# An HGRN2 recurrence in two groups of four heads, its output projection split over K, and overflow tables in whole passes

## What is computed

```python
def hgrn2(h, w_in, lb, o_norm_g, w_out):     # 8 heads of 128
    q, f, i, g = jnp.split(h @ w_in, 4, axis=-1)
    forget = lb + (1.0 - lb) * jax.nn.sigmoid(f)
    log_f, k, q = jnp.log(forget), 1.0 - forget, jax.nn.silu(q)
    ...
    def step(state, inp):                    # over chunks of 64 frames
        qc, kc, ic, lfc = inp
        b = jnp.cumsum(lfc, axis=2)
        o_inter = jnp.einsum('bhtk,bhkv->bhtv', qc * jnp.exp(b), state)
        ...
        o = o_inter + jnp.einsum('bhts,bhsv->bhtv', attn, ic)
        ...
    o = rms_norm(o, o_norm_g)                # per head
    return (o * jax.nn.silu(g)) @ w_out

x = x + rms_norm(mix, norm_g[layer, 1])
hn = rms_norm(x, norm_g[layer, 2])
logits = hn @ w_router + b_router            # then top 2 of 8, softmax, the experts
```

## Time and profile before

| | us |
|---|---|
| median of 3 runs | 1562.08 (1562.06 to 1563.52) |
| the profiled execution | 1561.03 |
| its span, first to last instruction | 1559.2 |
| TensorE busy | 1510.1 (97%) |
| DVE busy | 1277.6 (82%) |
| ACT busy | 1005.7 (64%) |
| DMA queue of the weights | 435.25 MB, 76.4% of 16 engines |

### The profile page before, as it was taken

How to read it: one execution, slowest core, us unless ns; L and a number is a source line. 1 busy time by engine, 2 the same in 40 slices (tenths; PEclk the granted TensorE clock), 3 DMA queues, 4 the chain that set the end, 5 groups by cost and what they waited for, 6 DMA issues and landing times.

```text
span 1559.2 us, 24123 instructions
## 1 busy us (share of the span) xinstructions
PE 1510.1 (97%) x7090; PEld 1257.1 (81%) x7101; DVE 1277.6 (82%) x1595; ACT 1005.7 (64%) x1274; POOL 10.7 (1%) x26
## 2 busy tenths in 40 slices
PE   7999999999979899999999999999999999999998
PEld 6777888788867688888888888888888888887876
DVE  6986455674877898999988989899999889998985
ACT  6555444464323577777767867777777777776772
POOL 1000000000000000000000000000000000000000
PEclk9999999999989899999999999999999999999999
DMA  7666555363322699989989989989989998998960
GB/s 279 205 226 216 190 185 185 114 217 119 111 81 95 246 365 368 366 330 371 353 327 381 355 329 372 370 310 380 377 307 379 379 349 330 372 351 330 378 259 28
DMA packets 121236, 439.93 MB, mean 282 GB/s; under 512 B 13664, under 2 KB 13664, under 8 KB 121200
## 3 DMA queue, kind: packets, MB, share of 16 engines
q1 hardware_dynamic: 119952, 435.25, 76.4%
q0 software_dynamic: 1248, 4.23, 0.7%
HBM read 438.38 MB, written 1.05 MB: 282 GB/s over the span
## 4 chain that ended last, share of the span: by engine, by line
PE 90%; DVE 6%; ACT 2%; issue 1%; DMA 1%; SPq 0%; DVEq 0%; ACTq 0%
PE PS L397 28%; PE PS L399 27%; PE PS L398 27%; DVE w_lo L1200 2%; PE PS L631 2%; PE PS L761 2%; PE PS L721 1%; DMA raw<-in_w_in_ab 1%; PE PS L735 1%; DVE xT_lo L1669 1%; ACT xT_hi L1106 0%; PE PS L736 0%; ACT w_hi L862 0%; PE PS L447 0%; ACT xT_hi L877 0%
## 5 line engine op out<-in xcount | busy, mean ns | idle before, releaser
L1200 DVE TENSOR_TENSOR w_lo<-raw,w_hi 128x1024 fp32r<-128x1024 f32 x486 | 567.8, 1221 | 34.4 <-ACT w_hi L862 31.5
L397 PE MATMUL PS<-w_hi,xT_hi 128*128 128x512 f32 x1424 | 566.1, 398 | 6.5 <-DVE xT_lo L1268 3.5
L399 PE MATMUL PS<-w_lo,xT_hi 128*128 128x512 f32 x1424 | 556.9, 391 | 0.0
L398 PE MATMUL PS<-w_hi,xT_lo 128*128 128x512 f32 x1424 | 555.9, 390 | 0.0
L862 ACT ACTIVATE w_hi<-raw 128x1024 fp32r<-128x1024 f32 x486 | 490.0, 1061 | 74.7 <-PE PS L399 49.1
L1200 DVE TENSOR_TENSOR w_lo<-SC,w_hi 128x1024 fp32r<-128x1024 f32 x340 | 391.3, 1220 | 11.5 <-ACT w_hi L862 10.5
L862 ACT ACTIVATE w_hi<-SC 128x1024 fp32r<-128x1024 f32 x340 | 337.5, 1060 | 34.2 <-PE PS L399 31.5
L397 PEld LDWEIGHTS PS<-w_hi,xT_hi 128*128 128x128 f32 x1424 | 269.3, 189 | 61.7 <-issue 3.9
L399 PEld LDWEIGHTS PS<-w_lo,xT_hi 128*128 128x128 f32 x1424 | 268.3, 188 | 57.7
L398 PEld LDWEIGHTS PS<-w_hi,xT_lo 128*128 128x128 f32 x1424 | 268.9, 189 | 53.6
L397 PE MATMUL PS<-w_hi,hT_hi 128*128 128x512 f32 x536 | 208.9, 390 | 4.1 <-DVE hT_lo L1405 4.1
(11 more groups left out here) (235 smaller groups left out, 722.9 us busy)
## 6 DMA issues: line engine op xcount, KB each, us to landing
raw<-in_e_w_gu SPq DMA_DIRECT2D x226, 512.0 KB, 6.7
SC<-in_e_w_gu SPq DMA_DIRECT2D x222, 512.0 KB, 6.7
SC<-in_e_w_down SPq DMA_DIRECT2D x114, 512.0 KB, 5.8
raw<-in_e_w_down SPq DMA_DIRECT2D x110, 512.0 KB, 6.2
raw<-in_ffn_w_gu SPq DMA_DIRECT2D x44, 512.0 KB, 4.8
raw<-in_w_in_c SPq DMA_DIRECT2D x32, 512.0 KB, 5.6
raw<-in_ffn_w_down SPq DMA_DIRECT2D x22, 512.0 KB, 5.0
raw<-in_w_in_ab SPq DMA_DIRECT2D x20, 512.0 KB, 6.9
```

The lines of the kernel that those rows point to most:

```text
L397: pe.matmul(out, a_hi, b_hi, start=start, stop=False, skip_group_check=True)
L398: pe.matmul(out, a_lo, b_hi, start=False, stop=False, skip_group_check=True)
L399: return pe.matmul(out, a_hi, b_lo, start=False, stop=stop, skip_group_check=True)
L1200: dve.tensor_tensor(w_lo[:, g % RING, part], raw_part(g, s), w_hi[:, g % RING, part].bitcast(F32), ALU.subtract).then_inc(lo_done, 1)
```

## The change

Four edits.

1. The eight heads are two groups of four (`GH` = 4), with their own buffers, semaphores (`qk_ready_low`, `qk_ready_high`) and PSUM banks. The chunks of the input projection come in the order f of group 0, q of group 0, f of group 1, q of group 1, values and gates of group 0, values and gates of group 1 (`INC`). The levels of group 0 begin behind half-granule 5, those of group 1 behind half-granule 9.
2. The output projection is split over K: the half of group 0 for both chunks is done first, that of group 1 last, tile by tile. `turn_x(3, 0)` stands behind all of it. A head norm now ends in four fused products per group and tile instead of two whole passes, and the loads of the experts' fourth granule wait for the last of four head norms.
3. The overflow tables are made for all three extra places at once.
4. `xT_half` without a scale copies and subtracts four blocks in one instruction.

```diff
+            proj(4)
+            pe.wait_ge(q_evac, 1)
+            turn_heads(q_nat[0], 6, qT_psum)
             proj(5)
+            pe.wait_ge(qT_act, 2)
+            level(0, 0)
+            proj(6)
+            level(0, 1)
...
+            proj(13)
+            across(0)
+            weigh_values(0, 0)
+            level(1, 4)
+            pe.wait_ge(g_evac, 1)
+            proj(14)
+            weigh_values(0, 1)
+            level(1, 5)
             proj(15)
-            level(7)
+            level(1, 6)
+            for t in range(T):
+                turn_o(0, t)
+            pe.wait_ge(i_evac, 2)
+            for t in range(T):
+                out_seg(0, 0, t)
+            level(1, 7)
             pe.wait_ge(g_evac, 2)
+            out_seg(0, 1, 0)
+            across(1)
+            weigh_values(1, 0)
+            out_seg(0, 1, 1)
+            weigh_values(1, 1)
             for t in range(T):
+                turn_o(1, t)
+                for c in range(2):
+                    out_seg(1, c, t)
+            turn_x(3, 0)
```

The helpers of TensorE that are new or changed:

```diff
+            def across(g):
+
+                pe.wait_ge(qk_ready[g], 9)
+                for hd in range(GH):
+                    m = pe.matmul(PS[:, o_bank(g, 1), hd * P:(hd + 1) * P], kT[g][:, hd, 0:P], qT[g][:, hd, P:SEQ],
+                                  start=True, stop=True, skip_group_check=True)
+                m.then_inc(at_done[g], 1)
+
+            def weigh_values(g, t):
+
+                pe.wait_ge(qk_ready[g], 9 + t)
...
+            def turn_o(g, t):
+
+                pe.wait_ge(o_ready, T * g + t + 1)
+                for j in range(HK):
+                    m = pe.transpose(PS[:, o_bank(g, t), j * P:(j + 1) * P], oo[g][:, t, j * P:(j + 1) * P], ident[:, :])
+                m.then_inc(xT_psum, 1)
+
+            def out_seg(h, c, t):
+                g = G_OUTC + 2 * h + c
+                pe.wait_ge(xT_ready, 8 * T + T * h + t + 1)
+                seg(g, c, h, t, h == 0, h == 1, None, h == 1)
```

DVE's order in the same stretch (`climb` is one level of one group, `norm_o` one head norm):

```diff
+            crossed(0)
+            gains_of(0)
+            climb(1, 4)
+            norm_o(0, 0)
+            lo(68)
+            climb(1, 5)
+            norm_o(0, 1)
+            lo(69)
+            climb(1, 6)
+            lo(70)
             for t in range(T):
+                oT(0, t)
+            climb(1, 7)
+            lo(71)
+            gains_of(1)
+            crossed(1)
+            norm_o(1, 0)
+            norm_o(1, 1)
+            oT(1, 0)
+            oT(1, 1)
+            los(72, 74)
             for c in range(2):
                 dve.wait_ge(y_half, Y_OUTC + c + 1)
                 weigh_psum(0, c, 4)
```

The head norm on DVE, the whole-half split, and the loads on SP:

```diff
+            def norm_o(g, t):
+
+                heads = slice(HEADS * g + GH * t, HEADS * g + GH * (t + 1))
+                dve.wait_ge(o_sq, T * g + t + 1)
+                step(dve.tensor_reduce(rt[:, heads], osq[g][:, t, :].rearrange("p (h n) -> p h n", n=HD), AXX, ALU.add))
+                step(dve.tensor_scalar(nr[:, 0, heads], rt[:, heads], 1.0 / HD, EPS, ALU.mult, ALU.add))
+                rsqrt(heads.start, heads.stop)
+                for hd in range(GH):
+                    cols = slice(hd * HD, (hd + 1) * HD)
+                    m = dve.scalar_tensor_tensor(out=oo[g][:, t, cols], in0=PS[:, o_bank(g, t), cols],
+                                                 scalar=nr[:, 1, heads.start + hd:heads.start + hd + 1],
+                                                 in1=gg[g][:, t, cols], op0=ALU.mult, op1=ALU.mult)
+                m.then_inc(o_ready, 1)
...
+                if v is None:
+                    part = (slice(None), slice(HK * b, HK * (b + 1)), slice(t * P, (t + 1) * P))
+                    dve.tensor_tensor(xT_lo[part], PS[:, tile_bank(t, final) + b, :].rearrange("p (k c) -> p k c", k=HK),
+                                      xT_hi[part].bitcast(F32), ALU.subtract).then_inc(xT_ready, 1)
+                    return
...
-            for c in (2, 3, 0, 1, 4, 5, 6, 7):
+            for c in INC:
...
-                        sp.wait_ge(o_ready, T)
+                        sp.wait_ge(o_ready, 2 * T)
```

ACT's order at the end, and the new table code:

```diff
+            by_tile(gg[1], PS[:, 2:4, :], ACT.Silu, 2, g_evac)
             for t in range(T):
+                oT(0, t)
+            hi(71)
+            hi(72)
+            for t in range(T):
+                square_o(1, t)
+            for t in range(T):
+                oT(1, t)
+            hi(73)
...
-            for j in range(XTRA):
-                step(dve.scalar_tensor_tensor(out=one, in0=place, scalar=float(j), in1=over, op0=ALU.is_equal, op1=ALU.mult))
-                step(dve.tensor_tensor(tmp, one, iota_c[:, 0:E], ALU.mult))
-                step(dve.tensor_reduce(head[:, 2 + j:3 + j], tmp, AXX, ALU.add))
-                for k, v in ((0, slot), (1, gates)):
-                    p3 = pair[:, 0:T, :]
-                    step(dve.tensor_tensor(p3, v.rearrange(tE, t=T), one.unsqueeze(1).broadcast_to([P, T, E]), ALU.mult))
-                    m = dve.tensor_reduce(tab[:, k, :, E + j + 1:E + j + 2], p3, AXX, ALU.add)
-                    step(m)
+            for k, v in ((0, slot), (1, gates)):
+                step(dve.tensor_tensor(moved, v.rearrange(tE, t=T).unsqueeze(1).broadcast_to(every),
+                                       which.unsqueeze(2).broadcast_to(every), ALU.mult))
+                step(dve.tensor_reduce(extra[:, k], moved, AXX, ALU.add))
+            emit(dve.tensor_reduce(head[:, 2:2 + XTRA], named, AXX, ALU.add))
```

More of the change, by code:

```diff
@@ L652, in _ @@
             proj(11)
-            level(3)
-            proj(12, (i_evac, 1))
-            level(4)
-            proj(13)
-            level(5)
-            proj(14, (i_evac, 2))
-            level(6)
-            proj(15)
-            level(7)
-            pe.wait_ge(qk_ready, 9)
-            for hd in range(HEADS):
-                m = pe.matmul(PS[:, 4 + hd // 4, (hd % 4) * P:(hd % 4 + 1) * P], kT[:, hd, 0:P], qT[:, hd, P:SEQ],
-                              start=True, stop=True, skip_group_check=True)
@@ L679, in turn_o @@
-            def turn_o(t):
-                pe.wait_ge(o_ready, t + 1)
-                for b in range(2):
-                    turn_half(oo, t, b)
-            turn_o(0)
-            tile_by_tile([(G_OUTC + n, OUT + n // 2, n % 2, n % 2 == 0, n % 2 == 1) for n in range(4)], 4 * T,
-                         [lambda: turn_o(1), lambda: turn_x(3, 0)], True)
+            level(0, 6)
+            level(1, 2)
+            pe.wait_ge(i_evac, 1)
+            proj(12)
+            level(0, 7)
+            level(1, 3)
@@ L1605, in _ @@
             m.then_inc(sel_ready, 1)
-            over, place, one, tmp = (rt[:, 336 + k * E:336 + (k + 1) * E] for k in range(4))
+            over, place = (rt[:, 336 + k * E:336 + (k + 1) * E] for k in range(2))
             step(dve.tensor_scalar(over, PS[:, 1, T * E:(T + 1) * E], float(P), None, ALU.is_gt))
```

333 lines of the change are left out of this document (187 added, 146 removed).

## The result

| kernel | median us | lowest to highest | runs |
|---|---|---|---|
| before | 1562.09 | 1561.73 to 1564.49 | 13 |
| changed | 1567.06 | 1565.66 to 1571.33 | 13 |

The ratio is 1.0034, with a 95% interval of 1.0025 to 1.0042: the change costs some 5 us, more than the 0.2% that a measurement tells here. The forecast was 1566.6 us (range 1556.0 to 1571.5) with "slower" the likeliest side.

The account below looks back on a forecast made before the run. TensorE, busy 1510.1 of 1559.2 us, was taken as the bound, winning only at pauses or low clock. The terms +6.5 + 1.0 - 2.7 - 0.3 = +4.5 us on the median 1562.08 gave 1566.6 us, range 1556 to 1571.5.

Parts of the forecast that it names:

- No pause up to 426.7: Recurrence up to the end of group 1's level 4: TensorE has 83.4 us of work from 343.3 and nothing waits.
- DVE's 24.3 us and the pause: Ahead of the first output segment: DVE needs 24.3 us, TensorE 17.2, so a new pause of 7.1 us arises.
- Rival C: End of the recurrence: DVE reaches `oT(0, 0)` in time, so pause and clock loss vanish; 1557.0 us, faster, chance 0.19.
- The three waits behind: Behind the first output segments, up to tile 0's x: TensorE also pauses 2.0, 4.2 and 1.4 us.
- The clock: Half clock behind TensorE's pauses: 2.5 us lost behind the 7.1 us pause, 1.6 behind the 2.0 + 4.2 us.
- Rival A: Behind the pauses and at the warming matmuls: clock barely moves, full rate; -0.6 us, 1561.5, chance 0.30.
- Rival B: Behind the pauses: clock stays low as long as before, 4.6 us more; 1571.2 us, chance 0.12.
- Rival D: First expert: tables win nothing since something else is late; 1569.3 us, chance 0.39 together with the forecast.
- x of tile 0, +6.5: Output projection's end: x of tile 0 stands at 494.4 against 487.93, +2.4 without clock loss, +6.5 with it.
- To the first expert, +1.0, bounds 0 and 2: From tile 0's x to the first expert matmul: warming matmuls may start at half clock, costing +1.0 us.
- Tables, -2.7: Overflow tables ahead of `hidden`: 28 small DVE operations become 15, -2.7 us, nothing for the clock, bounds -1.5 and -4.3.
- The splits, -0.3: Last gate: one copy and one difference replace halves of rows of four each, 0.3 us less; covered at the first gate.

Follow-up runs that it names:

- e1: Changed kernel with VectorE's `lo` granules 69 and 70 moved from ahead of `oT(0, 0)` and `oT(0, 1)` to behind them; 1563.42 us, +1.2 against before.
- e2: Changed kernel with `oT(0, 0)`, `oT(0, 1)` directly behind `norm_o(0, 1)`, ahead of group 1's level 6 and `lo` granules 69 and 70; 1559.86 us, -2.4 against before.
- e0: The changed kernel itself, unedited, measured and profiled once more; 1567.47 us, +4.5 against before.
- e11: Changed kernel with matmuls on zeros in TensorE's longer pauses between 444 and 502 us, no other engine's work moved; 1563.48 us, +1.1 against before.
- e4: Changed kernel with the overflow tables computed by the old loop of the kernel before; 1573.37 us, +11.1 against before.
- e5: Kernel before the change with only the new overflow tables in whole passes; 1558.06 us, -4.9 against before.
- e9: Changed kernel with 18 more matmuls on zeros behind `turn_x(3, 0)`, ahead of the router's small matmuls; 1566.92 us, +4.7 against before.

## Why the forecast was right, point by point

- **No pause up to 426.7.** TensorE leaves the first four granules at 343.70 (343.3 in the sum), and level 4 of group 1 ends at 426.67 (426.7). No pause of over 1 us stands between. The two more table loads cost nothing seen: behind those at 359.75 and 375.10 ScalarE still waits 5.00 us for TensorE.
- **DVE's 24.3 us and the pause.** Predicted 24.3 us of DVE's work from 426.7 and a pause of 7.1; measured 427.03 to 451.4 and 7.50. e1 and e2 confirm the cause: the two `lo` granules moved off (4.6 us) shorten the pause by 4.52. Level 6 moved off as well (3.0 us) shortens it by 1.96 only, since VectorE then waits 0.94 us for ScalarE. Rival C is refuted: the work was not shorter than taken (a head norm 3.94 us against 4.05).
- **The three waits behind.** 2.0, 4.2 and 1.4 us in the sum; 2.00, 3.65 and 1.41 measured (3.86 in e0).
- **The clock.** 2.5 and 1.6 us in the sum. In the first profile 9 matmuls behind the first pause and 13 behind the second stand at a pitch of 0.43 instead of 0.23: 1.8 and 2.6 us lost; in e0 it is 12 and 7, 2.4 and 1.4. So 3.8 to 4.4 against 4.1: right in size. Rival A (the clock barely moves) is refuted by the rows; that e11, with the clock kept, stands at +1.1 where A gave -0.6 tells that its sum was near, though e11's clock was kept in part only. Rival B's 4.6 us more did not come: behind the first pause 1.8 to 2.4 us were lost where B had 5. For the other two terms the first profile has B's sizes (2.6 and 2.04 against 2.7 and 2), e0 the forecast's (1.4 and 1.3). Rival D (the tables win nothing) falls with e4 and e5.
- **x of tile 0, +6.5.** Measured 496.08 against 487.93, +8.15; of the miss of 1.65 us 0.5 is the pause and 0.3 the clock (0.7 less than taken behind the first pause, 1.0 more behind the second), the rest small pieces of the walk. Two of the signs named in the forecast were missed by this: x of tile 0 two to seven us later, and, barely, the last projection matmul ending before 493 (it ends at 493.02). x of tile 1 follows by 12.9 us, as taken.
- **To the first expert, +1.0, bounds 0 and 2.** Measured +2.04, at its bound (e0: 528.05 - 510.10, +1.3). e9 shows that in the first profile all of it is the clock. The mechanism was right, the size low.
- **Tables, -2.7.** The size was low here too. The work shrank as counted (2.60 us from 532.24 to 534.84, against 5.7), and TensorE's wait by 3.09. But I wrote "nothing more for the clock", and the half clock behind the 5.86 us can go with the wait: e5's profile is 3.5 us shorter behind the first expert matmul, 0.4 more than the wait. e5's median, 4.9, lies beyond the bound of -4.3, its interval (3.1 to 6.1) does not.
- **The splits, -0.3.** The last gate's wait is 1.1 us where it was 1.43. Too small for a time of its own, and not tried by itself.

The total was 0.5 us off, and that is in part luck. By the profiles the first expert matmul comes 10.2 us later than before where the sum had +7.5 (the +6.5 and the +1.0), and what lies behind it is 3.7 us shorter (e0) where the sum had 3.0. Together that is +6.5, not +4.5. The medians differ by 4.5 to 5.0 only; the profiled execution of before is 1 us or more under its median, which is most of that gap. The two misses have opposite signs, and both have clock behind a wait in them that was left out or taken low: some 1.3 of the first 2.7 us, and about half of the other 0.7.

As for the rule weighed (the Trainium skill, VectorE: DVE Perf Modes, The TRN2 errata, on the fixed part exposed between instructions): the pause came out at 7.50 where the sum by the spacing had 7.1 and the page's full price would have made it an estimated 7.8. This does not decide it, but the spacing itself is again shorter than the duration: four `lo` halves of 1.22 us in 4.62.

## What to carry to other kernels

When work is split into groups so that TensorE need not wait, count the other engine's queue between two points of TensorE, item by item, and ask of each item ahead of the awaited one whether anyone needs it sooner: here four `lo` granules, one level and one head norm stood ahead of what TensorE waited for, and to move them (with one set of TensorE's transposes and one high half on ScalarE) turned +4.7 us into -10.8. What the split into groups is worth by itself stays open, since the kernel before was not reordered in the same way. The cost of a pause is its length and the clock behind it; put both into a sum, for the waits that go as for those that come. And profile a second execution before a difference of a few us is explained by its rows: the same program had a half clock behind the same pause in one execution and not in another.
